# The chunked state recurrence: one product of the state with wT and the gated queries, outputs on the other half of the partitions, inner part in PSUM banks of its own

## The reference, cut to what matters

```python
q = l2norm(heads(q))
k = l2norm(heads(k))
v = heads(v)
beta = jax.nn.sigmoid(beta_logit.astype(f32)).transpose(0, 2, 1)
g = (-jnp.exp(a_log.astype(f32)) * jax.nn.softplus(a_logit.astype(f32) + dt_bias.astype(f32))).transpose(0, 2, 1)
o = gated_delta_rule(q, k, v, g, beta).transpose(0, 2, 1, 3)
...
o = rmsnorm(o, dn_norm_w) * jax.nn.silu(zf)
```

## Time and profile before

| | us |
|---|---|
| three timed runs, median (lowest to highest) | 1498.23 (1496.36 to 1498.39) |
| the profiled execution, its time | 1495.34 |
| its span, first to last instruction | 1493.5 |
| PE busy | 1329.4 (89%) |
| VectorE busy | 859.4 (58%) |
| the recurrence on PE, first `kv` to the start of `pool_up` | 32.45 |

### The profile page before, as it was taken

How to read it: one execution, slowest core, us unless ns; L and a number is a source line. 1 busy time by engine, 2 the same in 40 slices (tenths; PEclk the granted TensorE clock), 3 DMA queues, 4 the chain that set the end, 5 groups by cost and what they waited for, 6 DMA issues and landing times.

```text
span 1493.5 us, 17435 instructions
## 1 busy us (share of the span) xinstructions
PE 1329.4 (89%) x6390; PEld 954.2 (64%) x6390; DVE 859.4 (58%) x1697; ACT 470.4 (31%) x807; POOL 651.2 (44%) x388
## 2 busy tenths in 40 slices
PE   5999998999989999999998797799778987787776
PEld 5998987998869988998775453344333443333332
DVE  3333243999137957331425766677677776777654
ACT  3564533443346333122001222222222232222211
POOL 5543246888856513220001543444344445444430
PEclk9999999999999999999999899999899998999998
DMA  7724333554534341211042999999999999999993
GB/s 267 287 84 172 113 143 120 195 195 169 208 131 154 143 184 63 108 57 57 7 191 106 423 421 422 421 421 421 422 421 421 421 421 421 421 421 421 422 421 127
DMA packets 50044, 389.90 MB, mean 261 GB/s; under 512 B 5144, under 2 KB 9384, under 8 KB 10024
## 3 DMA queue, kind: packets, MB, share of 16 engines
q0 software_dynamic: 36864, 268.45, 43.3%
q1 hardware_dynamic: 10560, 116.40, 20.7%
q10 hardware_dynamic: 2536, 3.95, 0.8%
HBM read 387.70 MB, written 1.07 MB: 260 GB/s over the span
## 4 chain that ended last, share of the span: by engine, by line
PE 60%; DMA 26%; DVE 6%; POOL 3%; issue 2%; ACT 1%; ACTq 0%; DVEq 0%; POOLq 0%
PE psum L488 59%; DMA work<-experts_dram,work 14%; DMA weight_ring<-experts_dram,work 10%; DVE work L1586 2%; DMA constants<-experts_dram,work 1%; POOL weight_lo L2036 1%; POOL work L2105 1%; PE psum L618 1%; ACT work L1972 0%; POOL norm_stats L2026 0%; DMA bias_rows_dram<-work 0%; ACT work L1655 0%; DVE residual L1097 0%; POOL weight_ring L2105 0%; ACT work L1800 0%
## 5 line engine op out<-in xcount | busy, mean ns | idle before, releaser
L488 PE MATMUL psum<-work 128*128 128x128 f32 (+6 forms) x1740 | 449.8, 413 | 87.1 <-ACT work L1972 81.3
L488 PEld LDWEIGHTS psum<-work 128*128 128x128 f32 (+2 forms) x1740 | 250.5, 191 | 275.3 <-issue 160.8
L2036 POOL TENSOR_TENSOR weight_lo<-weight_ring,weight_hi 128x2048 fp32r<-128x2048 f32 x64 | 299.7, 4683 | 182.5 <-ACT weight_hi L1655 159.4
L2105 POOL DMA_INDIRECT work<-experts_dram,work x154 | 175.6, 1140 | 238.3 <-PE psum L488 202.5
L1586 DVE CUSTOM_DVE_ANT_0 work<-work 128x1024 f32<-128x1024 f32 x154 | 189.0, 1227 | 113.8 <-DMA work<-experts_dram,work 99.1
L488 PE MATMUL psum<-weight_ring,work 128*128 128x512 f32 (+1 forms) x444 | 194.0, 585 | 29.6 <-ACT work L1972 29.5
L488 PEld LDWEIGHTS psum<-weight_ring,work 128*128 128x128 f32 (+1 forms) x444 | 81.0, 186 | 134.3 <-issue 83.2
L488 PE MATMUL psum<-normed_T,weight_ring 128*128 128x256 f32 (+1 forms) x768 | 159.3, 368 | 3.1 <-ACT normed_T L1655 1.9
L488 PEld LDWEIGHTS psum<-normed_T,weight_ring 128*128 128x128 f32 x768 | 138.3, 196 | 25.5 <-issue 6.9
L1655 ACT ACTIVATE weight_hi<-weight_ring 128x2048 fp32r<-128x2048 f32 x66 | 125.8, 1913 | 88.5 <-PE psum L488 48.3
L1972 ACT ACTIVATE work<-constants,work 128x128 f32<-128x128 f32 x256 | 102.8, 402 | 153.2 <-DVE work L1600 147.0
(11 more groups left out here) (257 smaller groups left out, 1692.3 us busy)
## 6 DMA issues: line engine op xcount, KB each, us to landing
weight_ring<-weights_dram SPq DMA_DIRECT2D x52, 2048.0 KB, 7.8
work<-experts_dram,work POOLq DMA_INDIRECT x154, 23.0
weight_ring<-weights_dram SPq DMA_DIRECT2D x2, 1024.0 KB, 13.2
gain_rows<-gains_dram SPq DMA_DIRECT2D x2, 1024.0 KB, 9.9
work<-bias_rows_dram ACTq DMA_DIRECT2D x2, 1024.0 KB, 10.3
weight_ring<-experts_dram,work POOLq DMA_INDIRECT x79, 19.9
constants<-constants_dram ACTq DMA_DIRECT2D x1, 1094.0 KB, 9.4
residual<-x_dram SPq DMA_DIRECT2D x1, 1024.0 KB, 5.3
```

The lines of the kernel that those rows point to most:

```text
L488: return nc.tensor.matmul(o, l, r, start=start, stop=stop)
L2036: G_.tensor_tensor(low, loaded, high.bitcast(F32), ALU.subtract).then_inc(S("weight_lo_ready"), 1)
L2105: G_.indirect_dma_start(out=slots[s], out_offset=None, in_=experts, in_offset=bass.IndirectOffsetOnAxis(ap=expert[:, n % UNIT_BUFS, i:i + ...
```

## The change

The state is multiplied once per chunk and head. A new buffer `wT_q` (one per tile of 128 tokens, laid in the places of `Dm` and `XT`) holds for each head four blocks of 64 columns: wT of the even chunk, gated queries of the even chunk, gated queries of the odd chunk, wT of the odd chunk. Two neighbouring blocks are one stationary operand of 128 columns, so that one product gives w S on the chunk's own partitions and (gated q) S on the other chunk's. The part that comes from `DTm` and the new values, now "inner", goes to banks of its own on the same other partitions, after both `kv`. Bank `o` is read by VectorE (the w S half, L1471 of the changed program) and by ScalarE (the query half). ScalarE copies inner of chunks 1 and 2 to `X`, and GpSimd adds it to `o_tok`; for the last chunk VectorE adds it from PSUM. Since the output now lies on the other chunk's partitions, the norms of q must too: `square_sums` for s >= 2 makes twice as many products, of 64 output partitions each. The transposes swap the chunks, which VectorE undoes with eight half operations in the place of four (L1503 before). The gating of the queries moves behind the last level of the solve.

```diff
@@ -253,3 +253,6 @@
     z_T = view(work, 6240 + 4096, HEADS, SEQ)
     o_tok = k_gated
+    wT_q = [view(work, lo, HEADS, 4, CHUNK) for lo in (16480, 2048)]
     dn_T = DTm.rearrange("p (a b) c -> p a (b c)", b=2)
@@ -788,3 +791,9 @@
                     for a in range(4):
-                        ins = mm(ps[:, 8 * t + 2 * a:8 * t + 2 * a + 2], square_buf[:, s % 2, a, t * P:(t + 1) * P], C("ones")[:, 0:2])
+                        cols = slice(8 * t + 2 * a, 8 * t + 2 * a + 2)
+                        if s < 2:
+                            ins = mm(ps[:, cols], square_buf[:, s % 2, a, t * P:(t + 1) * P], C("ones")[:, 0:2])
+                        else:
+                            for c in range(2):
+                                tokens = slice(t * P + c * CHUNK, t * P + (c + 1) * CHUNK)
+                                ins = mm(ps[(1 - c) * CHUNK:(2 - c) * CHUNK, cols], square_buf[:, s % 2, a, tokens], C("ones")[:, 0:2])
                 close_bank(ins, f"ssq{s}")
@@ -902,17 +911,22 @@
             pe.wait_ge(S("q_gated_ready"), 4)
+            def chunk_rows(c):
+                r = (c % 2) * CHUNK
+                return slice(r, r + CHUNK), slice(CHUNK - r, P - r)
             for c in range(N_CHUNKS):
-                t, r = c // 2, (c % 2) * CHUNK
-                rows = slice(r, r + CHUNK)
-                cols = slice(t * P + r, t * P + r + CHUNK)
-                if c > 0:
-                    for hg in range(2):
+                t = c // 2
+                rows, o_rows = chunk_rows(c)
+                for hg in range(2):
+                    if c > 0:
                         drained(pe, f"kv{c - 1}", hg)
-                        ps = open_bank(f"wS{c}", hg)
+                        ps = open_bank(f"o{c}", hg)
                         for a in range(4):
                             h = hg * 4 + a
-                            ins = mm(ps[rows, a * P:(a + 1) * P], XT[:, t * HEADS + h, rows], state[:, h, :])
-                        close_bank(ins, f"wS{c}", hg)
+                            ins = mm(ps[:, a * P:(a + 1) * P], wT_q[t][:, h, 2 * (c % 2):2 * (c % 2) + 2, :].rearrange("p c n -> p (c n)"),
+                                     state[:, h, :])
+                        close_bank(ins, f"o{c}", hg)
                 for hg in range(2):
                     if c > 0:
-                        drained(pe, f"wS{c}", hg)
+                        pe.wait_ge(S("new_values_ready"), 2 * (c - 1) + hg + 1)
                     if c < N_CHUNKS - 1:
@@ -923,10 +937,8 @@
                         close_bank(ins, f"kv{c}", hg)
-                    ps = open_bank(f"o{c}", hg)
+                for hg in range(2):
+                    ps = open_bank(f"inner{c}", hg)
                     for a in range(4):
-                        h = hg * 4 + a
-                        u = t * HEADS + h
-                        if c > 0:
-                            mm(ps[rows, a * P:(a + 1) * P], q_d[:, h, cols], state[:, h, :], True, False)
-                        ins = mm(ps[rows, a * P:(a + 1) * P], DTm[rows, u, rows], v_tok[rows, u, :], c == 0, True)
-                    close_bank(ins, f"o{c}", hg)
+                        u = t * HEADS + hg * 4 + a
+                        ins = mm(ps[o_rows, a * P:(a + 1) * P], DTm[rows, u, rows], v_tok[rows, u, :])
+                    close_bank(ins, f"inner{c}", hg)
             drained(pe, "pool", 1)
@@ -1426,9 +1438,2 @@
                 free(V.tensor_tensor(DTm[:, u, :], ps, DTm[:, u, :], ALU.mult), "kq", G)
-            for G in range(4):
-                u = slice(4 * G, 4 * G + 4)
-                t = G // 2
-                h0 = (G % 2) * 4
-                V.tensor_tensor(q_d[:, h0:h0 + 4, t * P:(t + 1) * P], q_d[:, h0:h0 + 4, t * P:(t + 1) * P], eR[:, u, :], ALU.mult)\
-                    .then_inc(S("q_gated_ready"), 1)
-                landed(dve, "q_gated_ready")
 
@@ -1450,2 +1455,8 @@
             for G in range(4):
+                u = slice(4 * G, 4 * G + 4)
+                t, h0 = G // 2, (G % 2) * 4
+                V.tensor_tensor(wT_q[t][:, h0:h0 + 4, 1:3, :].rearrange("p h c n -> p h (c n)"), q_d[:, h0:h0 + 4, t * P:(t + 1) * P], eR[:, u, :], ALU.mult)\
+                    .then_inc(S("q_gated_ready"), 1)
+                landed(dve, "q_gated_ready")
+            for G in range(4):
                 drained(dve, "u", G)
@@ -1458,4 +1469,5 @@
                     if c > 0:
-                        ps = full(dve, f"wS{c}", hg).rearrange("p (a n) -> p a n", a=4)
-                        free(V.tensor_tensor(v_tok[rows, u, :], v_tok[rows, u, :], ps[rows, :, :], ALU.subtract), f"wS{c}", hg)
+                        ps = full(dve, f"o{c}", hg).rearrange("p (a n) -> p a n", a=4)
+                        V.tensor_tensor(v_tok[rows, u, :], v_tok[rows, u, :], ps[rows, :, :], ALU.subtract).then_inc(S("new_values_ready"), 1)
+                        landed(dve, "new_values_ready")
                 if c < N_CHUNKS - 1:
@@ -1468,3 +1480,2 @@
                         else:
-                            full(dve, f"o{c}", hg)
                             for a in range(4):
@@ -1476,5 +1487,12 @@
 
-            for c in range(N_CHUNKS):
-                for hg in range(2):
-                    drained(dve, f"o{c}", hg)
+            c, o_rows = N_CHUNKS - 1, slice(0, CHUNK)
+            for hg in range(2):
+                u = slice((TT - 1) * HEADS + hg * 4, (TT - 1) * HEADS + hg * 4 + 4)
+                ps = full(dve, f"inner{c}", hg).rearrange("p (a n) -> p a n", a=4)
+                drained(dve, f"o{c}", hg)
+                free(V.tensor_tensor(o_tok[o_rows, u, :], ps[o_rows, :, :], o_tok[o_rows, u, :], ALU.add), f"inner{c}", hg)
+            for hg in range(2):
+                drained(dve, f"inner0", hg)
+                drained(dve, f"inner{c}", hg)
+            dve.wait_ge(S("o_added"), 2 * (N_CHUNKS - 2))
             for n in range(2):
@@ -1501,5 +1519,9 @@
             for i in range(4):
-                ps = full(dve, "dn_T", i).rearrange("p (a n) -> p a n", a=2)
-                free(V.scalar_tensor_tensor(out=dn_T[:, 2 * i:2 * i + 2, :], in0=ps, scalar=PR("dn_norm"), in1=z_T[:, 2 * i:2 * i + 2, :],
-                                            op0=ALU.mult, op1=ALU.mult), "dn_T", i)
+                ps, z, dst = (v.rearrange("p (b c n) -> p b c n", c=2, n=CHUNK) for v in
+                              (full(dve, "dn_T", i), z_T[:, 2 * i:2 * i + 2, :].rearrange("p a n -> p (a n)"),
+                               dn_T[:, 2 * i:2 * i + 2, :].rearrange("p a n -> p (a n)")))
+                for c in range(2):
+                    last = V.scalar_tensor_tensor(out=dst[:, :, c, :], in0=ps[:, :, 1 - c, :], scalar=PR("dn_norm"), in1=z[:, :, c, :],
+                                                  op0=ALU.mult, op1=ALU.mult)
+                free(last, "dn_T", i)
             drained(dve, "gate2_b0", 1)
@@ -1914,11 +1936,20 @@
                 ps = full(act, "wT", G)
-                free(copy(XT[:, u, :].rearrange("p a n -> p (a n)"), ps), "wT", G)
+                t, h0 = G // 2, (G % 2) * 4
+                free(copy(wT_q[t][:, h0:h0 + 4, 0::3, :], ps.rearrange("p (a c n) -> p a c n", a=4, c=2)), "wT", G)
             drain_gate("gate2_a1", gate_a2, 1)
             for c in range(N_CHUNKS):
-                t, r = c // 2, (c % 2) * CHUNK
-                rows = slice(r, r + CHUNK)
+                t, r = c // 2, CHUNK - (c % 2) * CHUNK
+                o_rows = slice(r, r + CHUNK)
+                for hg in range(2):
+                    u = slice(t * HEADS + hg * 4, t * HEADS + hg * 4 + 4)
+                    if c > 0:
+                        ps = full(act, f"o{c}", hg)
+                        free(copy(o_tok[o_rows, u, :].rearrange("p a n -> p (a n)"), ps[o_rows, :]), f"o{c}", hg)
                 for hg in range(2):
-                    ps = full(act, f"o{c}", hg)
                     u = slice(t * HEADS + hg * 4, t * HEADS + hg * 4 + 4)
-                    free(copy(o_tok[rows, u, :].rearrange("p a n -> p (a n)"), ps[rows, :]), f"o{c}", hg)
+                    dst = X if c else o_tok
+                    if c < N_CHUNKS - 1:
+                        ps = full(act, f"inner{c}", hg)
+                        free(copy(dst[o_rows, u, :].rearrange("p a n -> p (a n)"), ps[o_rows, :]), f"inner{c}", hg)
             def mixer_squares(t, half):
@@ -2085,2 +2116,11 @@
                     landed(pool, "level_L_ready")
+            for c in range(1, N_CHUNKS - 1):
+                t, r = c // 2, CHUNK - (c % 2) * CHUNK
+                o_rows = slice(r, r + CHUNK)
+                for hg in range(2):
+                    u = slice(t * HEADS + hg * 4, t * HEADS + hg * 4 + 4)
+                    drained(pool, f"o{c}", hg)
+                    drained(pool, f"inner{c}", hg)
+                    G_.tensor_tensor(o_tok[o_rows, u, :], o_tok[o_rows, u, :], X[o_rows, u, :], ALU.add).then_inc(S("o_added"), 1)
+                    landed(pool, "o_added")
             rstd(5, width=16)
```

## The result

The changed kernel takes **1482.26 us** (median of 4 runs, 1480.81 to 1483.78) beside 1498.05 (4 runs, 1496.36 to 1498.39) for the kernel before: a ratio of 0.9895, 95% interval 0.9879 to 0.9910. I had predicted 1486.9, with a range from 1484.5 to 1492.0: the sign and the mechanism of the recurrence held, and the gain, 15.8 us, was larger than the range allowed.

What follows compares the result with a forecast made beforehand. TensorE's chain, through the recurrence, was taken to set the start of the bandwidth-bound expert gather. Recurrence -12.1, square sums of q +0.6 and norm chain +0.2 gave -11.3 us: 1498.23 to 1486.9 us, range 1484.5 to 1492.0.

Steps and rivals of the forecast that it cites:

- The stage that counts: TensorE's chain up to the first gather sets the gather's start, which should come at about 803 in place of 814.
- Rival E: Something else, such as the weights, holds the gather's start, so the change does not reach the end: 1498.2 us; chance 0.04.
- The price of a product and of a switch: In the recurrence, 0.225 us per matmul and 0.14 us more per switch between kinds of matmul.
- The sum of 20.3: New recurrence: 18.0 for products, 1.4 for switches, 0.9 for waits, in place of 32.45 us, so -12.1 us.
- chunk 3's wait of 0.9: In the last chunk, without `kv`, TensorE waits 0.9 us for the new values before inner.
- The square sums of q: In q's square sums, 32 half loads take as long as 16 whole ones; two switches per bank add +0.6 us.
- My lower bound: For the cost of q's square sums: 0, if the switches vanish.
- Rival B: In q's square sums, half loads are as dear as whole ones: +3.6, 1490.5 us; chance 0.10.
- rival C: In q's square sums, alternating column halves costs a switch every time: +7.4 beyond the main forecast, 1494.3 us; chance 0.05.
- Behind the recurrence: The norm chain up to `dn_up0`: squares begin 0.05 later, L1503 in halves adds 0.1; together +0.2 us.
- At nothing: GpSimd's additions, the later gating of queries and ScalarE's copies of wT are hidden and cost nothing.
- rival D: In the recurrence, inner doesn't load ahead (1491.4) or VectorE and ScalarE take turns at a bank (1489.4); together 0.07.

Runs made afterwards that it cites:

- before_by_kind: The kernel before, with the recurrence's products of queries and inner part sorted by kind within each bank, all products kept: 1492.92 us, ratio 0.9970.
- squares_first: The changed kernel, with VectorE squaring and summing the first token tile ahead of the last chunk's two adds: 1484.79 us, one execution.

## Why the prediction was right, and where it failed

- **The stage that counts.** Right: the first gather came 11.7 us earlier (813.88 to 802.16). That this is so near the predicted 11.3 is in part luck: the change's own -12.5 came with -0.7, +1.4 and +0.1 from stretches without an edit. Rival E, that the change doesn't reach the end, is out.
- **The price of a product and of a switch.** Right: 0.225 and 0.14. before_by_kind isolates the second at 0.142. The sum of 20.3 met 20.42; chunk 3's wait of 0.9 is 0.90 in the row of the products and 1.06 in that of their loads; no product waits for a state update.
- **The square sums of q: the failed term.** "Then 32 loads at 0.056 take as long as 16 at 0.112" assumed that half loads queue behind each other. With one half after the other they do (1.73 us); in turns, as the change has them, two run side by side (1.01). +0.6 should have been -1.1: -1.7 for the two banks by the turns, and the changes of tile, which I had priced at 0.28 a bank, came out at 0.3. By this step the sum of -11.3 was 1.7 us short. My lower bound, "0, if the switches vanish", had no row that excluded a gain. Rival B (a half load as dear as a whole one) is out, and rival C weighed the same alternation as a cost only.
- **The rule that I passed over.** From the Trainium skill (TensorEngine Tiling (Array Packing), Key Properties) the prediction took the first rule, that a change of mode drains. The second says "Different tiles can execute LdWeights and Matmul in parallel", and it speaks for a gain in just this place. The trace agrees: 0.007 us between the loads of two halves, 1.01 us in turns beside 1.73 in sequence. The first rule holds as well: the Trainium skill (the same page, Tiling Modes) lists 64x128 and 64x64 as two configurations, and going from one to the other cost 0.16 us.
- **Behind the recurrence.** Right in kind, +0.6 for +0.2. "VectorE adds 0.69 after the same signal" sized the start too early. VectorE's second add begins 0.52 us behind the recurrence's end (719.00 less 718.48; its row has 0.54 us of waiting for TensorE), where ScalarE's copy had begun 0.17 behind it, and the squares follow after another 0.23: 1.43 us and not 0.94. Why the add begins that late isn't shown. The experiment squares_first puts 0.51 of the +0.6 there, and 0.13 on the gates in halves, for which I had 0.1.
- **At nothing.** Right: GpSimd's additions took 2.61 us a pair, more than the 1.09 each that I had taken, and still ended 2.1 us ahead of the recurrence's end; the stretch to the masks' end doesn't change with the gating moved.
- **The other half of the partitions** (rival D). Nothing is lost. Inner loads ahead (16 loads in 1.72 us), and ScalarE and VectorE read one bank at the same moment and both take their usual time (timeline of the changed kernel):

```profile
703.18 0.59 ACT L1677 ACTIVATE work<-psum 64x512 f32<-64x512 f32 x1 [0.50 <-PE psum L491]
703.19 0.69 DVE L1471 TENSOR_TENSOR work<-work,psum 64x512 f32<-64x512 f32 x1 [2.29 <-PE psum L491]
```

- **The range: failed too.** The measured time lies 2.2 us below its low end of 1484.5. By the change's own terms the time is 1498.05 - 12.5 = 1485.5, inside it; 1482.26 is 3.2 lower. Of that, 2.0 stand in the two profiles, in the stretches without an edit (-0.7, +1.4, +0.1, -2.8), and the rest is that the two profiled executions lie differently to their medians. None of it is shown to be the change's. The first timing gave a gain of 15.8, the two later ones of the same kernel 13.3 and 13.8. The interval of the first, 13.5 to 18.1 us, doesn't hold 12.5; those of the two later, 10.3 to 15.3 and 10.9 to 16.0, do. I had allowed for too little scatter: the kernel before itself ran from 1494.2 to 1500.9 within one timing. In the level section a single half-clock stretch makes 1.4 us; the cause of the larger part stays open. The low end should have lain about 2 us lower for that, and 1.7 for the missed gain.

## What to carry to other kernels

Count the changes of tile in TensorE's list as well as its products: sorted by kind, the old recurrence gave up 5 of 32 us with no work removed. Where outputs fill only half of the partitions, put the halves in turns, product by product: two narrow products then take the time of one, but a group must be long enough to pay about 0.3 us for going in and out, and it pays only until TensorE has to wait for another engine. And when a bound of an unknown cost is set at zero, name the row that excludes a gain.

## What the runs showed of the hardware

- Two matmuls that read the same 64 rows (or all 128) and write different column halves overlap nearly whole: 32 loads in 1.01 us for 1.73, and in the recurrence 16 loads and their products in 1.02 us for 1.89 (first load of the group to the first of the next), with 128 columns to move in each.
- A change of tile costs 0.14 to 0.16 us, whether the rows change (128 to 64) or the columns (64x128 to 64x64); from 128x128 to 128x64 the first load comes 0.2 us late (0.33 for 0.12).
- In one execution, in a list of products with such a gap after each, the granted clock stood at 0.50 in place of 1.00 for 20.5 us in all, while TensorE counts as busy throughout.
- One half-clock stretch of 3.4 us costs 1.4 to 1.6 us where TensorE sets the time (level section, 99.7 and 101.1 to 101.3), and falls or doesn't fall in the same place of the same kernel from run to run.
